# Half chunks of 1 MB in the ring of expert weights of a hybrid encoder

## The reference, cut to what matters

```python
def expert_choice_ffn(h, w_router, w_gate, w_up, w_down):
    b, s, _ = h.shape
    cap = EC_CAPACITY * s // N_EXPERTS           # 2 * 512 / 16 = 64 tokens for each expert
    aff = jax.nn.softmax((h @ w_router).astype(jnp.float32), axis=-1)
    gates, idx = lax.top_k(jnp.swapaxes(aff, 1, 2), cap)
    b_idx = jnp.arange(b)[:, None, None]
    xe = h[b_idx, idx]
    hid = (jax.nn.silu(jnp.einsum('becd,edf->becf', xe, w_gate))
           * jnp.einsum('becd,edf->becf', xe, w_up))
    ye = jnp.einsum('becf,efd->becd', hid, w_down) * gates[..., None].astype(h.dtype)
    return jnp.zeros_like(h).at[b_idx, idx].add(ye)
```

## Time and profile before

| | us |
|---|---|
| median of three runs | 2063.83 |
| the three runs | 2061.94, 2066.13, 2063.83 |
| the profiled execution, its own time | 2066.95 |
| its span, first to last instruction | 2065.2 |
| PE busy | 1869.3 (91%) |
| DVE, ACT, POOL busy | 833.6, 516.3, 237.2 |
| moved by DMA | 460.98 MB, of which 450.28 MB read from HBM |

### The profile page before, as it was taken

How to read it: one execution, slowest core, us unless ns; L and a number is a source line. 1 busy time by engine, 2 the same in 40 slices (tenths; PEclk the granted TensorE clock), 3 DMA queues, 4 the chain that set the end, 5 groups by cost and what they waited for, 6 DMA issues and landing times.

```text
span 2065.2 us, 43988 instructions
## 1 busy us (share of the span) xinstructions
PE 1869.3 (91%) x19446; PEld 991.5 (48%) x19446; DVE 833.6 (40%) x1676; ACT 516.3 (25%) x1000; POOL 237.2 (11%) x293
## 2 busy tenths in 40 slices
PE   6799999999998967999998889899985899998888
PEld 4366766766767533333333336566543333333332
DVE  6655664654754232222221203677724122222211
ACT  2243453443343110111101003455521011101010
POOL 1033023123113110000000001111111000000000
PEclk9899999999999987999999999999998899999999
DMA  4001101101103549999999990300036999999997
GB/s 120 14 23 37 43 8 37 43 8 37 43 8 117 186 175 376 428 427 427 427 428 427 427 413 7 114 23 23 11 134 258 371 427 427 427 428 427 427 427 316
DMA packets 85287, 460.98 MB, mean 223 GB/s; under 512 B 16741, under 2 KB 49898, under 8 KB 60522
## 3 DMA queue, kind: packets, MB, share of 16 engines
q1 hardware_dynamic: 82794, 449.78, 53.5%
q0 software_dynamic: 2304, 8.39, 1.0%
HBM read 450.28 MB, written 7.86 MB: 222 GB/s over the span
## 4 chain that ended last, share of the span: by engine, by line
PE 59%; DMA 21%; DVE 7%; issue 5%; ACT 3%; DVEq 2%; SPq 1%; POOL 0%; POOLq 0%; ACTq 0%; PEldq 0%; another core or an unknown queue 0%
DMA arena<-in_moe_w_down 17%; PE banks L1593 13%; PE bank L539 8%; PE banks L1309 5%; PE banks L820 4%; PE bank L1593 4%; PE bank L1639 3%; DMA arena<-in_moe_w_up 2%; ACT arena L2126 2%; PE banks L924 2%; PE banks L1639 2%; PE banks L1007 1%; PE banks L944 1%; PE banks L798 1%; PE banks L2087 1%
## 5 line engine op out<-in xcount | busy, mean ns | idle before, releaser
L1593 PE MATMUL banks<-arena 128*64 128x512 f32 x2560 | 568.8, 597 | 27.0 <-DMA arena<-in_moe_w_up 14.9
L1593 PEld LDWEIGHTS banks<-arena 128*64 128x64 f32 x2560 | 180.2, 137 | 379.3 <-issue 347.5
L1698 DVE TENSOR_TENSOR arena<-arena,bank 128x512 f32<-128x512 f32 x80 | 55.0, 687 | 321.7 <-PE bank L1639 321.7
L539 PE MATMUL bank<-arena 128*128 128x512 f32 x336 | 165.9, 616 | 1.3 <-DVE arena L1237 0.7
L1155 POOL TENSOR_TENSOR arena<-arena 128x512 f32<-128x512 f32 x80 | 101.6, 1296 | 475.6 <-DVE arena L1212 475.6
L1593 PE MATMUL bank<-arena 128*64 128x512 f32 x512 | 119.1, 616 | 25.6 <-DMA arena<-in_moe_w_down 25.6
L820 PE MATMUL banks<-arena 64*64 64x64 f32 x5632 | 126.9, 222 | 12.0 <-DVE arena L1237 5.9
L820 PEld LDWEIGHTS banks<-arena 64*64 64x64 f32 x5632 | 112.0, 135 | 51.2 <-issue 36.1
L1652 ACT ACTIVATE arena<-banks 128x512 f32<-128x512 f32 x32 | 19.1, 597 | 413.5 <-PE banks L1593 413.5
L1687 DVE SCALAR_TENSOR_TENSOR arena<-arena,banks 128x512 f32<-128x512 f32 x32 | 33.7, 1052 | 206.6 <-PE banks L1593 206.6
L1309 PE MATMUL banks<-arena 128*128 128x512 f32 x256 | 112.6, 594 | 1.8 <-POOLq L399 1.3
(11 more groups left out here) (343 smaller groups left out, 2597.9 us busy)
## 6 DMA issues: line engine op xcount, KB each, us to landing
arena<-in_moe_w_gate SPq DMA_DIRECT2D x64, 2048.0 KB, 36.3
arena<-in_moe_w_up SPq DMA_DIRECT2D x64, 2048.0 KB, 38.3
arena<-in_moe_w_down SPq DMA_DIRECT2D x60, 2048.0 KB, 38.8
out_dram<-arena SPq DMA_DIRECT2D x12, 512.0 KB, 2.6
arena<-in_x SPq DMA_DIRECT2D x8, 512.0 KB, 5.2
arena<-in_rw_wr SPq DMA_DIRECT2D x8, 512.0 KB, 3.9
arena<-in_rw_wk SPq DMA_DIRECT2D x8, 512.0 KB, 5.9
arena<-in_rw_wv SPq DMA_DIRECT2D x8, 512.0 KB, 6.2
```

Source lines behind the costliest of these rows:

```text
L539: last = nc.tensor.matmul(b[:, :], w_sl[:, n, k, :], xmix[n][:, k, :], start=(k == 0), stop=(k == ND - 1))
L1593: last = nc.tensor.matmul(b[z * CAP:(z + 1) * CAP, :], st[:, k, :], ring[g % RING][:, k, z * 512:(z + 1) * 512], start=(c % 2 == 0 and k = ...
L1698: nc.vector.tensor_tensor(xs, xs, b[:, :], ALU.add).then_inc(free[COMB[j]], 1)
```

## The change

Each chunk but the last is loaded by two DMAs of 1 MB, for k = 0, 1 and k = 2, 3, each with its own semaphore (`ld_half[slot][n]`, which replaces `ld_chunk[slot]` and two of the six `ld_piece`). PE waits at k = 0 and at k = 2. From chunk 10 on, the first half of a slot is refilled when PE has read the first half of the chunk ten before: every chunk now counts up `half_used` at k = 1, and `half_read` waits for g + 1. The second half is refilled when that chunk is read to its end. The last chunk stays in quarters, two behind each of these waits. PE does the same matmuls in the same order.

```diff
--- before.py
+++ after.py
@@ -359,9 +359,9 @@
         ld_wo = [sem(f"ld_wo{n}") for n in range(2)]
         ld_router = [sem(f"ld_router{n}") for n in range(2)]
         ld_gcol = [sem(f"ld_gain_columns{n}") for n in range(2)]
-        ld_chunk = [sem(f"ld_chunk{s}") for s in range(RING)]
-        ld_piece = [sem(f"ld_piece{n}") for n in range(6)]
-        half_used = [sem(f"first_chunk_half_used{n}") for n in range(2)]
+        ld_half = [[sem(f"ld_chunk{s}_half{n}") for n in range(2)] for s in range(RING)]
+        ld_piece = [sem(f"ld_last_quarter{n}") for n in range(4)]
+        half_used = [sem(f"chunk_half_used{n}") for n in range(2)]
         ld_win = sem("ld_win")
         ld_mla = sem("ld_mla")
         ld_pair2 = sem("ld_pair2")
@@ -1537,22 +1537,16 @@
         xjs = [Jobs(order, oj.count) for oj in ojs]
         h_dram = a["out"][0]
 
-        FIRST_REFILL, LAST_CHUNK = RING, CPP * PAIRS - 1
-        PIECES = {FIRST_REFILL: [(0, slice(0, 2)), (1, slice(2, 4))], LAST_CHUNK: [(2 + k, slice(k, k + 1)) for k in range(4)]}
-
-        def whole_chunks(s, end):
-
-            return len([g for g in range(s, end, RING) if g not in PIECES])
+        LAST_CHUNK = CPP * PAIRS - 1
+        HALVES = [slice(0, 2), slice(2, 4)]
 
         def arrived(pe, layer, g, k):
 
             s = g % RING
-            if g in PIECES:
-                for n, ks in PIECES[g]:
-                    if ks.start == k:
-                        pe.wait_ge(ld_piece[n], 16 * (layer + 1))
-            elif k == 0:
-                pe.wait_ge(ld_chunk[s], (whole_chunks(s, g + 1) + whole_chunks(s, CPP * PAIRS) * layer) * 16)
+            if g == LAST_CHUNK:
+                pe.wait_ge(ld_piece[k], 16 * (layer + 1))
+            elif k % 2 == 0:
+                pe.wait_ge(ld_half[s][k // 2], 16 * (len(range(s, g + 1, RING)) + len(range(s, LAST_CHUNK, RING)) * layer))
 
         def rows_pe(pe, i, layer):
             xj = xjs[layer]
@@ -1593,7 +1587,7 @@
                             last = nc.tensor.matmul(b[z * CAP:(z + 1) * CAP, :], st[:, k, :],
                                                     ring[g % RING][:, k, z * 512:(z + 1) * 512],
                                                     start=(c % 2 == 0 and k == 0), stop=(c % 2 == 1 and k == 3))
-                        if g == 0 and k == 1:
+                        if k == 1:
                             last.then_inc(half_used[layer], 1)
                     last.then_inc(full[xj[name][0]] if c % 2 else chunk_used[layer], 1)
 
@@ -1703,15 +1697,21 @@
             e, r = divmod(c, 4) if c < 8 else ((c - 8) // 2, 4 + c % 2)
             w, h = (("moe_w_gate", 0), ("moe_w_gate", 1), ("moe_w_up", 0), ("moe_w_up", 1), ("moe_w_down", 0), ("moe_w_down", 1))[r]
             src = a[w][layer][2 * i + e, h * 512:(h + 1) * 512, :].rearrange("(p k) n -> p k n", k=4)
-            if g not in PIECES:
-                sp.dma_start(ring[g % RING], src).then_inc(ld_chunk[g % RING], 16)
-                return
-            for n, ks in PIECES[g]:
-                if g == FIRST_REFILL and n == 0:
-                    sp.wait_ge(half_used[layer], 1)
-                elif n < 3:
-                    chunk_read(sp, layer, g - RING)
-                sp.dma_start(ring[g % RING][:, ks, :], src[:, ks, :]).then_inc(ld_piece[n], 16)
+            for n, ks in enumerate(HALVES):
+                if g >= RING:
+                    half_read(sp, layer, g - RING, n)
+                if g < LAST_CHUNK:
+                    sp.dma_start(ring[g % RING][:, ks, :], src[:, ks, :]).then_inc(ld_half[g % RING][n], 16)
+                else:
+                    for k in range(2 * n, 2 * n + 2):
+                        sp.dma_start(ring[g % RING][:, k:k + 1, :], src[:, k:k + 1, :]).then_inc(ld_piece[k], 16)
+
+        def half_read(sp, layer, g, n):
+
+            if n == 0:
+                sp.wait_ge(half_used[layer], g + 1)
+            else:
+                chunk_read(sp, layer, g)
 
         def chunk_read(sp, layer, g):
             xj = xjs[layer]
```

## The result

The changed kernel takes 2072.41 us in the median of ten runs (2069.02 to 2075.55), against 2064.51 (2061.94 to 2068.22) of the kernel before: a ratio of 1.0039 with a 95% interval of 1.0031 to 1.0047. It is slower by 7.9 us, clear of noise, where the forecast was 2065.6, too little to be told from no change. The time lies within 1 us of the slower rival's 2071.5.

The account below looks back on a forecast made before the run. It took the expert stages to be bound by a DMA stream at 427 GB/s. Packets +6.7, start -2.5 and end -2.4 gave +1.8 us on 2066.95, or 2065.6 on the median's scale; 8 in 10 range 2058 to 2073.

Parts of the forecast that it names:

- slower rival: Packets cost 0.06 us a chunk, +10.1, the start's dip stays, only -2.4 comes off: +7.7, 2071.5 us; 25%.
- What bounds the kernel: Expert stages are a DMA stream at 427 GB/s; refills matter only at a stage's start, arrivals only at its end.
- Step (a): Stream of chunks 11 to 94: more packets from halves cost 0.04 us a chunk, +6.7 us, ends +1.7 and +10.1.
- second look: Packet price from the last chunk's quarters: nothing extra in layer 1, 0.1 to 0.2 us more in layer 0.
- Step (b): Start of a stage: chunk 11's first half issued earlier, so the queue's dip goes; -2.5 us, bounds 0 and -5.0.
- Step (c): End of a stage: PE reads chunk 94 by halves and ends 1.3 us sooner; -1.2 each, -2.4 us.
- theory C: Layer 0's end: waits between quarters let PE's clock fall in the adds, +0.7 in place of -1.1; sum -0.4 us.
- Step (d): PE's 84 further waits a layer, semaphore increments, SP's second issues and the first gather beside chunk 8: 0 us.
- rivals of +84 and -27 us: +84: each transfer shows its own start-up, 1%. -27: SP's waits are real, earlier refills shorten ring cycles, 2%.

Follow-up runs that it names:

- e9_late_refill: The changed kernel, but both halves of a slot wait until the chunk ten before is read to its end; 2074.13 us, 1.0058 against the kernel before.
- e2_quarters: The changed kernel with every chunk in four DMAs of 512 KB (4 KB rows), two on each half's semaphore; 2099.86 us, 1.0170 against the kernel before.
- e4_tail: The kernel before with only chunk 94 beside 10 in halves, a wait each, refilled together; 2063.03 us, 1.0000 against the kernel before.
- e5_edges: The kernel before with only chunks 10 to 13 (refilled half by half) and 94 in halves; 2060.33 us, 0.9985 against the kernel before.

## Why the prediction was right and wrong

**What bounds the kernel** was right. The stage is a stream; the refills by halves took 385 us off a row of SP's waits and gave nothing in the stream, and e9_late_refill shows it by itself.

**Step (a), the packets,** is where it failed. The term was +6.7 us, at 0.04 a chunk with an upper end of 0.06; in the profiles it is 5.9 us a layer over 83 chunks, 0.071 each, or +11.9 over 168. The mechanism was right, and its price was too low by almost half. I had the price from two stretches that don't belong together: 4 KB packets at 418 GB/s in a 6 us stretch of another load, and 16 KB packets at 427 in the stream. In the stream itself 4 KB packets make 409, as e2_quarters shows: at 409 a row of 16 KB takes 640.9 ns, at 427 613.9, 9.0 ns for each of three further packets and not 4.4. Packets are cheaper in a fresh stretch, for 16 KB as well (607.1 for 611.0), and 4.4 is near the price there (2 x 306.0 for 8 KB less 607.1 is 4.9).

The second look, at the last chunk's quarters, had two faults. I added 0.1 us for PE's pickup in layer 0 and not in layer 1; by the landings, chunk 94 to the last quarter is 5.07 us in layer 0 and 4.96 in layer 1. At the stream's price four quarters take 4.91 + 0.22 = 5.1, so layer 0 had it right, and I let layer 1 pull the price down. In layer 0 the loads of the next layer stand behind the last chunk. In layer 1 nothing does, and most engines are done before the slowest, so that a landing there is not the stream's pace. In the kernel before, the last 3.6 us ahead of the landing at 2050.6 move 88 GB/s:

```profile
DMA packets 86, 0.32 MB, mean 88 GB/s; under 512 B 12, under 2 KB 12, under 8 KB 85
```

The upper end of 0.06 was thereby no bound.

The Trainium skill's rule of three cycles for each packet (DMA: Bandwidth & Descriptors, "Why small descriptors are slow (HBM only)") makes an estimated 0.6% of halves and 1.7% of quarters. This case measures 1.4% to 1.5% and 4.3% of the stream (5.9 and 6.3, and 18.4, on 423.2 us). So a fixed time in each packet is what the runs show too, and the rule's size is under half of the measured one.

**Step (b), the start:** right in kind and in place. Its size was -2.5, and in the two main profiles the dip shrinks by just that (6.3 and 6.1 us to 5.0 and 5.0). Over all stages with and without it the difference is 0.8 to 0.9 a layer, some -1.8: the one profile had larger dips than the mean of ten stages.

**Step (c), the end:** -1.3 worked out, 1.1 measured in both layers (from 2.15 and 2.26 us behind the last quarter to 1.12). In layer 0 of the changed kernel it was given back: the first of PE's adds after it ran at half their speed,

```profile
1240.11 1.97 PE L1633 MATMUL bank<-arena 128*128 128x512 f32 x2 [1.49 <-ACTq L1655]
1241.87 1.89 PE L1633 MATMUL banks<-arena 128*128 128x512 f32 x2
```

for 1.10 us in layer 1, in a window with a granted clock of 0.66:

```profile
1240.00:1245.00 5.00, 4.89 (x8) 2.14 (x9) 1.72 (x3) 0.48 (x1) 0.00 (x0) 0.66 0.84 314
```

That is 1.7 us in this one execution: layer 1's first projection starts 13.9 us after the last quarter's landing. e2_quarters, e4_tail, e5_edges and e9_late_refill have the same waits between the last pieces, 1.10 us for the same two matmuls, and 12.2. So the waits alone don't bring it on, and theory C of e4_tail fell; the kernel before has stretches of 3.4 us at a granted clock of 0.50 too, from 1109.6 and from 1171.1 us, inside the stream. What brings them on is not shown.

**Step (d), at nothing:** held. SP's issues, now 2 to 3 us long in a full queue, hid as the ones before did, and the small loads between the layers still came with the stream's end. The first gathers took 5.23 and 5.02 us in the chain, for 5.65 and 4.45.

**The sum** of the measured parts is +11.9 - 1.8 - 2.2 = +7.9 us, for a measured difference of 7.9 between the medians; the parts come from single profiles and are good to some tenths each. The slower rival had this time (+7.7), and half of its reason: the packets cost more than its +10.1, but the gain of the start, which it gave up, stayed. That its two misses cancel is luck. The time also lies inside the range only because that reached to 2073 for this rival's sake: the term of the packets, +11.9, ended outside the bounds of +1.7 and +10.1 that I had given it.

**The rivals of +84 and -27 us** fell: one DMA or two for the same 8 KB rows gave the same stream, and a later refill in the stream cost nothing. The 2 us that the prediction takes from the Trainium skill (DMA: Bandwidth & Descriptors, "Anatomy of one DMA") are given there for DMAs that GpSimd issues; these come from SP, and no run here measures theirs apart.

## What to carry to other kernels

In a stream that kept the DMA engines full, as here, what splitting a transfer cost was its number of packets. Take that price from packets in such a stream and not from a short stretch or from its tail, and split only the few chunks where something waits (here 2 or 4 more of 96 in a layer: -0.14% and -0.15% in place of +0.39%). Waits of the issuing queue said nothing about the stream while more was queued than it needed; three chunks of 2 MB were enough here, two were not.

## What was not expected

- A fixed cost of some 8.4 ns in each packet beside its bytes, which grows out of some 5 ns in the first 25 to 35 us of a stage (16 KB: 607.1 to 611.0 ns; 8 KB: 306.0 to 309.7). It is the same with three chunks queued and without the seven later gathers; its cause is open.
- A second DMA for the same bytes costs nothing that shows: 8 KB rows in one DMA or in two gave the same stream, 429.5 and 429.0 us a layer.
- The queue takes about 27 us of halves (eleven transfers of 1 MB), and SP then stands in its issues; with whole chunks it took up to ten of 2 MB.
